# Compressed attention branch: a stacked first product, and output products among its scores

## The reference, cut to what matters

```python
def _compress(a, pe, w1, b1, w2, b2):
    ...
    blocks = (blocks + pe).reshape(B, G, nc, CMP_LEN * dk)
    return jax.nn.gelu(blocks @ w1 + b1) @ w2 + b2
...
k_cmp = _compress(to_g(kc), pe[0], w1[0], b1[0], w2[0], b2[0])
v_cmp = _compress(to_g(vc), pe[1], w1[1], b1[1], w2[1], b2[1])
...
sc = jnp.einsum('bgrqd,bgcd->bgrqc', qc, k_cmp)
p_cmp = _masked_softmax(sc, cmp_end[None, :] <= t[:, None])
o_cmp = jnp.einsum('bgrqc,bgcd->bgrqd', p_cmp, v_cmp)
...
mixed = _head_rmsnorm(jnp.concatenate([conv_out, attn_out], -1), head_norm_g[i])
x = _layer_norm(ALPHA * x + mixed @ w_out[i], ln1_g[i], ln1_b[i])
```

## Time and profile before

| what | value |
|---|---|
| median of three runs | 710.58 us |
| the profiled execution's own time | 709.42 us |
| its span, first to last instruction | 707.6 us |
| TensorE busy | 690.6 us (98%), 4822 products |
| VectorE, ScalarE, GpSimd busy | 492.1 us, 345.1 us, 158.6 us |
| mean granted TensorE clock | 0.985 of full |
| DMA | 116.85 MB, 165 GB/s |

### The profile page before, as it was taken

How to read it: one execution, slowest core, us unless ns; L and a number is a source line. 1 busy time by engine, 2 the same in 40 slices (tenths; PEclk the granted TensorE clock), 3 DMA queues, 4 the chain that set the end, 5 groups by cost and what they waited for, 6 DMA issues and landing times.

```text
span 707.6 us, 11957 instructions
## 1 busy us (share of the span) xinstructions
PE 690.6 (98%) x4822; PEld 631.8 (89%) x4822; DVE 492.1 (70%) x698; ACT 345.1 (49%) x492; POOL 158.6 (22%) x54
## 2 busy tenths in 40 slices
PE   8999999999999999999999999999999999999995
PEld 5899999888999999999778999988889999999994
DVE  4675768877996666666786457686869766666646
ACT  5654535414865444444347444453258555555520
POOL 0000020230174444440000000113106444444300
PEclk9999999899999999999999999997999999999998
DMA  9972443333875555556248143432357755555301
GB/s 290 323 249 62 142 156 119 120 119 106 282 241 195 191 195 196 194 188 179 78 148 269 61 150 118 152 102 78 119 200 245 269 179 179 179 178 178 119 0 60
DMA packets 87403, 116.85 MB, mean 165 GB/s; under 512 B 5230, under 2 KB 73536, under 8 KB 87360
## 3 DMA queue, kind: packets, MB, share of 16 engines
q1 hardware_dynamic: 85920, 111.85, 47.3%
q10 hardware_dynamic: 1440, 4.39, 1.8%
HBM read 115.19 MB, written 1.05 MB: 164 GB/s over the span
## 4 chain that ended last, share of the span: by engine, by line
PE 92%; DVE 5%; DMA 1%; issue 1%; ACT 1%; SPq 0%; DVEq 0%; ACTq 0%
PE bank L1154 28%; PE bank L1155 27%; PE bank L1156 27%; PE bank L1239 3%; PE bank L1226 2%; DMA x_tok<-in_x 1%; PE bank L1175 1%; DVE x_tok L941 1%; DVE stats L925 1%; DVE x_tok L923 1%; PE bank L1218 1%; DVE ring_lo L290 1%; DVE x_tok L949 1%; PE bank L1328 1%; PE bank L1305 0%
## 5 line engine op out<-in xcount | busy, mean ns | idle before, releaser
L290 DVE TENSOR_TENSOR ring_lo<-raw,ring_hi 128x2048 fp32r<-128x2048 f32 x102 | 232.5, 2284 | 21.6 <-ACT ring_hi L286 21.5
L1154 PE MATMUL bank<-xh,ring_hi 128*128 128x256 f32 x832 | 237.6, 286 | 0.0
L1156 PE MATMUL bank<-xh,ring_lo 128*128 128x256 f32 x832 | 235.8, 283 | 0.0
L1155 PE MATMUL bank<-xl,ring_hi 128*128 128x256 f32 x832 | 235.7, 283 | 0.0
L286 ACT ACTIVATE ring_hi<-raw 128x2048 fp32r<-128x2048 f32 x102 | 194.4, 1909 | 11.9 <-DMA raw<-in_w_in 9.1
L693 POOL COPY step_par<-ffn_par 128x16 f32 (+1 forms) x22 | 127.5, 5800 | 170.9 <-DVE work L962 170.9
L1154 PEld LDWEIGHTS bank<-xh,ring_hi 128*128 128x128 f32 x832 | 159.8, 192 | 0.9
L1155 PEld LDWEIGHTS bank<-xl,ring_hi 128*128 128x128 f32 x832 | 159.8, 192 | 0.6
L1156 PEld LDWEIGHTS bank<-xh,ring_lo 128*128 128x128 f32 x832 | 159.7, 192 | 0.0
L962 DVE SCALAR_TENSOR_TENSOR work<-bank,step_par,work 128x255 f32<-128x255 f32 (+1 forms) x176 | 72.2, 474 | 95.2 <-ACT work L532 95.1
L532 ACT ACTIVATE work<-bank,step_par 128x256 f32<-128x256 f32 x88 | 44.2, 560 | 117.1 <-PE bank L1156 117.1
(11 more groups left out here) (178 smaller groups left out, 785.6 us busy)
## 6 DMA issues: line engine op xcount, KB each, us to landing
raw<-in_w_up SPq DMA_DIRECT2D x44, 1024.0 KB, 5.2
raw<-in_w_down SPq DMA_DIRECT2D x22, 1024.0 KB, 5.3
raw<-in_w_in SPq DMA_DIRECT2D x21, 1024.0 KB, 5.2
raw<-in_cmp_w SPq DMA_DIRECT2D x8, 1024.0 KB, 5.9
raw<-in_w_out SPq DMA_DIRECT2D x8, 1024.0 KB, 4.9
qkv<-in_ln_g ACTq DMA_DIRECT2D x4, 512.0 KB, 3.4
qkv<-in_ln_b ACTq DMA_DIRECT2D x4, 512.0 KB, 4.9
raw<-in_w_in SPq DMA_DIRECT2D x2, 512.0 KB, 5.6
```

What stands on the lines that cost most here:

```text
L290: eng.tensor_tensor(ring_lo[slot_of(L, u)][:], raw[raw_of(L, u)][:], ring_hi[slot_of(L, u)][:].bitcast(fp32), ALU.subtract).then_inc(split ...
L1154: pe.matmul(dst, ah, bh, start=start, stop=False, **kw)
L1155: pe.matmul(dst, ah, bl, start=False, stop=False, **kw)
L1156: return pe.matmul(dst, al, bh, start=False, stop=stop, **kw)
```

## The change

It has two parts.

The first stacks the compression's first layer. `ring_hi` and `ring_lo` become the two halves of one `ring` tile, and for the four `w1` units the splits write high and low rows of 256 in turn, so that a slice's high and low weights stand side by side as 512 columns. The blocks' high and low parts stand side by side as 60 stationary columns. One product of 512 columns then makes all four combinations (low by low too, which was not made before), in place of three of 256. The result is 60 rows by 512, which ScalarE copies whole. The four parts are added up on the way through TensorE: in place of each transpose there are two fp32 products, one with a stacked identity (60 by 30, new in the constants), one with the plain identity.

The second reorders the end of attention. After every second head of the compressed scores one `out_product` of the first token tile is made (four in all, what `out_part(L, 0, 0, 0)` and `out_part(L, 0, 0, 1)` were), and the second token tile's two parts stand ahead of `transpose_cmp`, behind the wait for the compressed scores' maxima, since they write the bank from which those are read.

```diff
--- before.py
+++ after.py
@@ -84,6 +85,7 @@
+    c[0:2 * NG * NBLK, C_ST:C_ST + NG * NBLK] = np.tile(np.eye(NG * NBLK), (2, 1))
@@ -138,14 +140,15 @@
-        ring_hi = [sb(f"ring_hi{i}", [P, UNIT], f32r) for i in range(SLOTS)]
-        ring_lo = [sb(f"ring_lo{i}", [P, UNIT], f32r) for i in range(SLOTS)]
+        ring = [sb(f"ring{i}", [P, 2 * UNIT], f32r) for i in range(SLOTS)]
+        ring_hi, ring_lo = ([r[:, UNIT * n:UNIT * (n + 1)] for r in ring] for n in range(2))
+        ring_rows = [r[:].rearrange("p (k a n) -> p k a n", k=8, a=2) for r in ring]
...
-        hid = sb("hid", [NG * NBLK, CMP_HID])
+        hid = sb("hid", [2 * NG * NBLK, 2, CMP_HID])
...
@@ -283,12 +287,18 @@
-            nc.scalar.activation(ring_hi[slot_of(L, u)][:], raw[raw_of(L, u)][:], ACT.Copy).then_inc(hi_done, 1)
+            dst, src = ring_hi[slot_of(L, u)], raw[raw_of(L, u)][:]
+            if u in W1_U[0] + W1_U[1]:
+                dst, src = ring_rows[slot_of(L, u)][:, :, 0], src.rearrange("p (k n) -> p k n", k=8)
+            nc.scalar.activation(dst, src, ACT.Copy).then_inc(hi_done, 1)
...
@@ -468,7 +478,8 @@
-                nc.scalar.activation(hid[:], bank[2 + kv][0:NG * NBLK, 0:CMP_HID], ACT.Copy).then_inc(hid_copied, 1)
+                nc.scalar.activation(hid[:].rearrange("p a n -> p (a n)"), bank[2 + kv][0:2 * NG * NBLK, :],
+                                     ACT.Copy).then_inc(hid_copied, 1)
@@ -1246,19 +1257,20 @@
-                    wh, wl = w_view(L, u, 8)
                     for j in range(8):
                         k = 8 * half + j
-                        ins = mm3(bank[2 + kv][0:NG * NBLK, 0:CMP_HID], blocks_h[kv][:, k, :], blocks_l[kv][:, k, :],
-                                  wh[:, j, :], wl[:, j, :], k == 0, k == NJ - 1)
+                        ins = pe.matmul(bank[2 + kv][0:2 * NG * NBLK, :].rearrange("p (a n) -> p a n", a=2), blocks_r[kv][:, k].rearrange("p a b -> p (a b)"),
+                                        ring_rows[slot_of(L, u)][:, j], start=k == 0, stop=k == NJ - 1)
...
                 for h in range(2):
-                    ins = pe.transpose(bank[2 + kv][:, 256 + 32 * h:286 + 32 * h], hid[:, P * h:P * (h + 1)],
-                                       ident[0:NG * NBLK, 0:NG * NBLK])
+                    dst = bank[2 + kv][:, 256 + 32 * h:286 + 32 * h]
+                    pe.matmul(dst, hid[:, 0, P * h:P * (h + 1)], cst[0:2 * n, C_ST:C_ST + n], start=True, stop=False)
+                    ins = pe.matmul(dst, hid[0:n, 1, P * h:P * (h + 1)], ident[0:n, 0:n], start=False, stop=True)
@@ -1287,7 +1299,11 @@
-                ins.then_inc(s_done, 1)
+                        if h == NPAIR - 1 and t == TT - 1:
+                            ins.then_inc(s_done, 1)
+                        if h % 2:
+                            wait_mix(L, 0, t)
+                            out_product(L, 0, h // 2, t)
@@ -1577,7 +1593,7 @@
-                        out_part(L, 0, 0, 0)
+                        wait_unit(L, U_OUT)
                         mean_squares(L, 1)
                         cmp_scores(L)
@@ -1592,14 +1608,14 @@
-                out_part(L, 0, 0, 1)
+                pe.wait_ge(exp_done, N_ATT * L + 12)
+                pe.wait_ge(max_done, N_ATT * L + 13)
+                out_part(L, 1, 0, 0)
+                out_part(L, 1, 0, 1)
                 transpose_cmp(L)
                 conv_roots(L, 1)
                 times_v_cmp(L, 0)
                 times_v_cmp(L, 1)
-                pe.wait_ge(exp_done, N_ATT * L + 13)
-                out_part(L, 1, 0, 0)
-                out_part(L, 1, 0, 1)
                 out_unit(L, 0, 1)
```

More of the change, by code:

```diff
@@ L64 @@
 C_MA, C_M01, C_BM, C_BLK = 320, 350, 380, 388
-C_ALL = C_BLK + 2
+C_ST = C_BLK + 2
+C_ALL = C_ST + NG * NBLK
 def shape_constants():
@@ L146, in build @@
         xl = sb("xl", [P, KT, SEQ], f32r)
-        hTh = sb("hTh", [P, 2, 2, SEQ], f32r)
-        hTl = sb("hTl", [P, 2, 2, SEQ], f32r)
+        hT = sb("hT", [P, 2, 2, 2, SEQ], f32r)
+        hTh, hTl = hT[:, 0], hT[:, 1]
         qTh = sb("qTh", [P, NPAIR, SEQ], f32r)
@@ L214, in build @@
         last_hTh, last_hTl = qTh[:, 0:2, :], qTl[:, 0:2, :]
-        blocks_h, blocks_l = ([a[:, kv].rearrange("p c n -> p (c n)")[:, 0:480].rearrange("p (j b) -> p j b", j=NJ)
-                               for kv in range(2)] for a in (hTh, hTl))
+        blocks_r = [hT[:].rearrange("p a k c n -> p (a k c n)")[:, 1024 * kv:1024 * kv + 960]
+                    .rearrange("p (j a b) -> p j a b", j=NJ, a=2) for kv in range(2)]
+        blocks_h, blocks_l = ([r[:, :, a] for r in blocks_r] for a in range(2))
         roots_h, roots_l = (a[:].rearrange("p a (t c) n -> p a t (c n)", t=TT) for a in (hTh, hTl))
@@ L285, in split_hi @@
             act.wait_ge(slot_free[slot_of(L, u)], CREDIT + slot_round(L, u, i))
-            nc.scalar.activation(ring_hi[slot_of(L, u)][:], raw[raw_of(L, u)][:], ACT.Copy).then_inc(hi_done, 1)
+            dst, src = ring_hi[slot_of(L, u)], raw[raw_of(L, u)][:]
+            if u in W1_U[0] + W1_U[1]:
+                dst, src = ring_rows[slot_of(L, u)][:, :, 0], src.rearrange("p (k n) -> p k n", k=8)
+            nc.scalar.activation(dst, src, ACT.Copy).then_inc(hi_done, 1)
         def split_lo(eng, L, u, i=0):
             eng.wait_ge(hi_done, L * NU + u + 6 * i + 1)
-            eng.tensor_tensor(ring_lo[slot_of(L, u)][:], raw[raw_of(L, u)][:], ring_hi[slot_of(L, u)][:].bitcast(fp32),
-                              ALU.subtract).then_inc(split_done[raw_of(L, u)], 1)
+            lo, hi, src = ring_lo[slot_of(L, u)], ring_hi[slot_of(L, u)], raw[raw_of(L, u)][:]
+            if u in W1_U[0] + W1_U[1]:
+                lo, hi = (ring_rows[slot_of(L, u)][:, :, a] for a in (1, 0))
+                src = src.rearrange("p (k n) -> p k n", k=8)
+            eng.tensor_tensor(lo, src, hi.bitcast(fp32), ALU.subtract).then_inc(split_done[raw_of(L, u)], 1)
         def bcast(ap, axis, shape):
@@ L1258, in transpose_hidden @@
                 settled(pe)
+                n = NG * NBLK
                 for h in range(2):
-                    ins = pe.transpose(bank[2 + kv][:, 256 + 32 * h:286 + 32 * h], hid[:, P * h:P * (h + 1)],
-                                       ident[0:NG * NBLK, 0:NG * NBLK])
+                    dst = bank[2 + kv][:, 256 + 32 * h:286 + 32 * h]
+                    pe.matmul(dst, hid[:, 0, P * h:P * (h + 1)], cst[0:2 * n, C_ST:C_ST + n], start=True, stop=False)
+                    ins = pe.matmul(dst, hid[0:n, 1, P * h:P * (h + 1)], ident[0:n, 0:n], start=False, stop=True)
                 ins.then_inc(hidT_done, 1)
```

## The result

The changed kernel takes 724.76 us (715.68 to 725.98, six runs); the kernel before, measured beside it, 711.41 (708.83 to 713.85, six runs). The ratio is 1.0166, 95% interval 1.0122 to 1.0210. The forecast was 706.0 with a range up to 712. The six runs go with their mean clock: four at 0.965 to 0.967 took 724.2 to 726.0 us, two at 0.978 and 0.980 took 717.0 and 715.7.

The account below looks back on a forecast made before the run. It took TensorE's own program as the bound, except VectorE's run at the end of attention. Savings of 3.5 + 0.9 = 4.4 us took the profiled 709.42 to 705.0, 706.2 on the median's scale; forecast 706.0, range 703.5 to 712.

Parts of the forecast that it names:

- End of attention: First wide product to VectorE's copy of the last transposed probabilities takes 7.0 us; the whole step saves 0.9 us.
- Rival 2: The clock still falls among the compressed scores: about 712 us, or 708.5 to 709.5 in one layer only; chance 0.2.
- VectorE's run: End of attention, from the last transposed probabilities' copy to scaling the second tile's heads: 14.62 us in both layers.
- the twelve products ahead of `transpose_cmp`: The second tile's moved output products, 2.7 us, are hidden because the softmax ends 4.15 us after VectorE's copy.
- The new wait: TensorE waits 2.2 us ahead of the first heads' transposes, released by VectorE, costing nothing in the sum.
- Rival 3: The clock falls at the wait of 2.2 us and dense output products run at half clock: 714.6 us; chance 0.08.
- First part: The compression's stacked first layer, keys and values, saves 3.5 us over both layers.
- the values' first layer: Sixteen products of 512 columns take 3.64 us in place of 5.58, 1.9 us less.
- the turn: Transposing `hid` by four fp32 products in the compression takes 0.81 us, 0.6 more than before.
- The wait behind unit 14: In the values' first layer TensorE waits about a microsecond for ScalarE's `hid` copy, behind a split waiting for its load.
- without the wait: Rival case without the wait behind unit 14: first part saves 4.8 us, in all 5.7, giving 704.9; chance 0.14.
- rival 4: The first part gives back its saving through a costlier wide product or slower split writes: 709 to 711 us; chance 0.08.

Follow-up runs that it names:

- e10: e6 with two dummy products ahead of the mean squares in place of six: 713.63 us, ratio 1.0073.
- e6: e2 with six dummy products of 512 columns ahead of the mean squares: 713.53 us, ratio 1.0057.
- e13: The whole change plus two dummy products of 512 columns ahead of the mean squares: 712.54 us, ratio 1.0058.
- e2: The changed kernel with the compression's first layer as before, so only the reordered end of attention: 724.61 us, ratio 1.0225.
- e3: e2 with the second token tile's output products back behind `times_v_cmp`: 721.02 us, ratio 1.0165.
- e4: The kernel before with only the second token tile's output products moved ahead of `transpose_cmp`: 713.91 us, ratio 1.0066.
- e7: The kernel before with twelve dummy products of 512 columns ahead of `transpose_cmp`, nothing moved: 714.42 us, ratio 1.0070.
- e5: e2 with six wide products again ahead of the mean squares, the other six among the second tile's scores: 715.63 us, ratio 1.0056.
- e14: e2 with four dummy products of 256 columns behind the last score: 720.25 us, ratio 1.0143.
- e1: The changed kernel with the end of attention as before, so only the stacked first layer and interleaved splits: 708.91 us, ratio 1.0016.
- e8: e1 with the keys' turn of `hid` between the parts of `conv_unit(2)` and the values' behind `scores(2)`: 717.24 us, ratio 1.0107.
- e9: e8 with VectorE's low part of unit 11 made ahead of `maxima(1)`: 707.44 us, ratio 0.9969.
- e11: e9 with the keys' turn of `hid` straight behind `scores(1)`, where the change puts it: 707.63 us, ratio 0.9972.

## Why the prediction was wrong, step by step

**End of attention: the step that failed.** It read "Afterwards that stretch holds 0.81 ... I take 7.0", at full clock. The sum of the terms was right: e10 measured 7.00. With the change as made it was 12.59 and 12.12, since the clock fell at once and the wide products, counted at 0.227, took 0.43. I had seen in the earlier trace rows that narrow work came ahead of the fall, and counted the mixture as dense. What I didn't count is what the change takes away: the six wide products that stood ahead of the mean squares (125.56 to 127.03; from the first of them to the fall it was 4.7 us in the kernel before). e6, e10 and e13 show that dense work in that place, even unused, brings most of the time back.

**Rival 2** was this mechanism, but mis-sized: it let the fall come "as far into the stretch as before" and priced 6.2 us over both layers. The fall came after 0.5 us in layer 0 and 1.1 in layer 1, and lasted 17 us where it had lasted 6.66 and 10.20. Of the 15.6 us of e2, e3 puts some 12 on it.

**VectorE's run "then takes 14.62"**: 15.94 and 16.42. The text held the twelve products ahead of `transpose_cmp` to be hidden, 2.7 us in a gap of 4.15. They were partly at half clock (141.69 to 145.48, 3.79), behind 3.28 of times_v at half clock, and `transpose_cmp` came 1.32 late for VectorE. e4 and e7 show that this place has no slack with the order before and its fall: what is added there is paid in full. That the transposes of the heads come right behind VectorE's scaling had been read as VectorE being the bound. But in the kernel before TensorE has no wait there either, and VectorE's copy at 137.81 came straight behind `transpose_cmp`: the two engines were level, and a delay of either counts. At full clock the step holds (e10: 14.43).

**The new wait**: 1.86 us instead of 2.2, in another place and for another reason. It stands ahead of `out_unit(0, 1)` and waits for VectorE's `mix_conv_low(1)` (L920), which `out_part(1, 0, *)` had covered. I had looked for the next wait at the heads only. Rival 3's mechanism, the fall behind the wait, came in both layers with some 3.3 us at half clock each, 6.6 of the 16.9 us that the rival took. The prediction also held that the wait "costs nothing in this sum". It stands in every version with tile 1's products early (e2, e4, e5, e6, e10, e13, e14 and the changed kernel) and in none of the others; that move costs about 5 us in e4, and about 4 stay where the clock holds (e10). It is the smaller part of the loss, and a second term that was mis-sized, at nothing.

**First part.** Right: the values' first layer took 3.77 us (73.61 to 77.38) against 5.58, 1.8 less, predicted 1.9. Mis-sized: the turn took 1.33, not 0.81; its records stand 0.166 apart, not 0.10, with 30 columns where the row I took had 2. That is 1.1 lost per turn, not 0.6, 2.1 more over four turns. The wait behind unit 14 was there, 0.63 us per layer where I had about one; but not for the load: in e1 the two splits follow each other without a gap, from ScalarE's copy of the compressed keys on. The load was the cause only in e8, where the turn came later; there and in e9 the chain as I had described it was shown. Not foreseen: the clock falls behind the keys' turn, 3.4 us, by an estimate (half of it) 1.7 us of loss in e1's one fall and in each layer of the changed kernel. The account for e1: 2.8 less 1.3 of waits less 1.7 is nothing, where I had 3.5. Two slips were in the sum itself: without the wait it is 3.2 less 0.6, 2.6 per layer and 5.2 in all, not 4.8; and the load was let come only 0.2 later for the longer turn, where the text's own term is 0.6, which makes the first part 2.7. That product and splits stay as fast as assumed (1.9 and 2.3 us per split) was right; rival 4 gave the right outcome of this part for the wrong cause.

On the clock, the Trainium skill, TensorE: Matmul & The Clock Gate, Part 1, says that the monitor runs freely and isn't in step with the kernel, so that the same kernel differs from run to run; it says so of the first products of a kernel. Carried over to the falls on the way, it makes them a matter of odds; the traces agree, with the two layers of e5 and of e14, and with mean clocks of 0.973 to 0.993 for the kernel before in one series of runs.

## What to carry to other kernels

Before taking dense products away from in front of narrow ones, ask what TensorE will then have done just before them, and price the stretch, and everything unhidden in it, at both levels of the clock. Two dummy products of 0.2 us ahead of a narrow stretch are a cheap test of that. Two engines that end level are both the bound: moving work of one ahead of what the other waits for is not free (e4). When a step moves later, follow it through the other engines' queues down to the loads (e8), and find out with dummies whether a place has slack (e7) before counting on it.

The first part is worth having only with its queues put right: e9 and e11 have medians 3 us below before's, but their intervals reach 1.0004 and 1.0008, so a gain is likely and not shown.

## What the runs showed of the hardware

Work added to TensorE's program made a kernel 11 us faster (e2 to e6). The time of a run follows its mean clock: the kernel before took 706.6 us at 0.991, 709.1 at 0.985 and 713.9 at 0.978. In e2 (layer 1), e3, e5 and e8 (layer 0) and e14 (layer 1) the clock fell at a wait of 0.64 us that stands in the kernel before too, whose profile stayed at 1.00 there; in e8 the order behind it is that of before. What decides in a given run stays open. An fp32 product with 30 columns takes 0.33 us as two records, with 2 columns 0.20; the two transposes of the kernel before, also of 30 columns, took 0.21 together.
